# Seven half-size products in place of eight for two blocks of a mixer's input projection

## The reference, cut to what matters

```python
h = rmsnorm(x, norm_mix_g)
gq, gk, gv, gz, gb, ga, sB, sC, sx, cq, ck, cv = split_cols(h @ w_in)
...
u, sc_buf_new = causal_dwconv(sC * sx, sc_buf, sc_conv_w)
y_b = group_rmsnorm(sB * u, SC_GROUPS, sc_norm_g).astype(dt)
```

## Time and profile before

| | us |
|---|---|
| median of 3 runs | 930.41 (930.28 to 930.81) |
| the profiled execution | 930.92 |
| its span in the profile | 929.2 |
| TensorE busy in the span | 918.9 |
| VectorE busy | 651.8 |
| ScalarE busy | 443.0 |
| GpSimd busy | 164.6 |

### The profile page before, as it was taken

How to read it: one execution, slowest core, us unless ns; L and a number is a source line. 1 busy time by engine, 2 the same in 40 slices (tenths; PEclk the granted TensorE clock), 3 DMA queues, 4 the chain that set the end, 5 groups by cost and what they waited for, 6 DMA issues and landing times.

```text
span 929.2 us, 16790 instructions
## 1 busy us (share of the span) xinstructions
PE 918.9 (99%) x6895; PEld 835.2 (90%) x6895; DVE 651.8 (70%) x1060; ACT 443.0 (48%) x793; POOL 164.6 (18%) x195
## 2 busy tenths in 40 slices
PE   8999999999999999999999999999999999999998
PEld 7899888999988877798788999999999998888886
DVE  6726888866888755743667999999999998445321
ACT  7634454645675543645554534444444445333310
POOL 0072101101845330000002222122222220000000
PEclk9999999999999999999999999999999999999999
DMA  9624143124204183345705222222222224312221
GB/s 322 214 89 147 47 157 117 47 74 145 87 4 136 65 265 123 121 152 209 245 1 204 92 74 69 86 92 91 91 91 92 86 65 182 108 68 91 90 80 57
DMA packets 75490, 106.34 MB, mean 114 GB/s; under 512 B 2798, under 2 KB 54166, under 8 KB 75030
## 3 DMA queue, kind: packets, MB, share of 16 engines
q1 hardware_dynamic: 75414, 105.27, 33.8%
HBM read 94.89 MB, written 10.37 MB: 113 GB/s over the span
## 4 chain that ended last, share of the span: by engine, by line
PE 91%; DVE 4%; ACT 3%; issue 1%; DMA 1%; POOL 1%; SPq 0%; DVEq 0%; ACTq 0%
PE bank L1274 8%; PE bank L1272 8%; PE bank L1273 8%; PE bank L558 6%; PE bank L559 6%; PE bank L560 6%; PE bank L519 6%; PE bank L520 6%; PE bank L521 6%; PE bank L487 5%; PE bank L584 2%; PE bank L585 2%; PE bank L586 2%; PE bank L505 2%; PE bank L507 2%; PE bank L506 2%
## 5 line engine op out<-in xcount | busy, mean ns | idle before, releaser
L2236 DVE TENSOR_TENSOR wlo<-wraw,whi 128x2048 fp32r<-128x2048 f32 (+1 forms) x56 | 126.1, 2252 | 100.3 <-ACT whi L1681 91.7
L1681 ACT ACTIVATE whi<-wraw 128x2048 fp32r<-128x2048 f32 (+1 forms) x58 | 109.3, 1885 | 95.4 <-PE bank L560 70.2
L519 PE MATMUL bank<-hhi,whi 128*128 128x320 f32 x352 | 115.3, 328 | 0.0
L521 PE MATMUL bank<-hhi,wlo 128*128 128x320 f32 x352 | 108.7, 309 | 0.0
L520 PE MATMUL bank<-hlo,whi 128*128 128x320 f32 x352 | 108.7, 309 | 0.0
L519 PEld LDWEIGHTS bank<-hhi,whi 128*128 128x128 f32 x352 | 66.2, 188 | 4.1 <-issue 2.6
L520 PEld LDWEIGHTS bank<-hlo,whi 128*128 128x128 f32 x352 | 66.2, 188 | 1.6 <-issue 1.0
L521 PEld LDWEIGHTS bank<-hhi,wlo 128*128 128x128 f32 x352 | 66.1, 188 | 0.0
L558 PE MATMUL bank<-whi,hhi 128*128 128x512 f32 x150 | 58.4, 389 | 0.0
L559 PE MATMUL bank<-wlo,hhi 128*128 128x512 f32 x150 | 58.4, 389 | 0.0
L560 PE MATMUL bank<-whi,hlo 128*128 128x512 f32 x150 | 58.3, 389 | 0.0
(11 more groups left out here) (501 smaller groups left out, 2657.6 us busy)
## 6 DMA issues: line engine op xcount, KB each, us to landing
wraw<-in_w_in SPq DMA_DIRECT2D x13, 1024.0 KB, 5.5
wraw<-in_w_gate SPq DMA_DIRECT2D x11, 1024.0 KB, 5.1
wraw<-in_w_up SPq DMA_DIRECT2D x11, 1024.0 KB, 5.2
wraw<-in_w_down SPq DMA_DIRECT2D x10, 1024.0 KB, 5.0
kTs<-in_cache_sb_k SPq DMA_DIRECT2D x8, 512.0 KB, 4.7
vraw<-in_cache_sb_v SPq DMA_DIRECT2D x8, 512.0 KB, 5.1
wraw<-in_w_mix_out SPq DMA_DIRECT2D x4, 1024.0 KB, 7.6
kmT<-in_cache_mem_k SPq DMA_DIRECT2D x8, 512.0 KB, 6.1
```

What stands on the lines that cost most here:

```text
L519: T.matmul(o, wh[:, k, cs], hhi[:, k, hs], start=(k == 0), stop=False)
L521: ins = T.matmul(o, wl[:, k, cs], hhi[:, k, hs], start=False, stop=(k == KD - 1))
L1681: V(wv(whi, i), wv(wraw, i), ACT.Copy).then_inc(s["w_hi_ready"], 1)
L2236: V.tensor_tensor(wv(wlo, i), wv(wraw, i), wv(whi, i).bitcast(F32), ALU.subtract)\
```

## The change

Each 1024 x 256 product is cut into halves of depth, of columns and of tokens, and formed by seven products of quarters (Winograd's form of Strassen's scheme) in place of eight: four of them use sums of quarters of the weights or of the tokens. Such a product is 4 steps of k by 3 matmuls. The sums and their own high and low parts are new work for VectorE and ScalarE, and the seven results are added on VectorE. The four token sums overwrite `xT`, so TensorE's gates, which read it, move ahead of the second half of `cq`. The key and value caches for the first samples are loaded later, since the sums of the `sx` weights lie where they would land. GpSimd's list is the same.

TensorE, the seven products and their order (`FRONT_STEPS`), two steps a unit:

```diff
+        FRONT_ORDER = (2, 1, 0, 3)
+        FRONT_STEPS = (("p1", "00"), ("p7", "p6"), ("p5", "01"), ("10",))
...
+"front": (2, 6, 7), "wide": (0, 1, 2, 6, 7), "turns": (3, 4, 5, 0, 1)
...
-            across(("cq", 0), B_CQ, hhi, hlo, ready=lambda c, k: pe.wait_ge(s["hlo_ready"], k + 1) if c == 0 else None)
+            across(("cq", 0), B_CQ, hhi, hlo, cs=(0,), ready=lambda c, k: pe.wait_ge(s["hlo_ready"], k + 1))
...
+            ring[0] = "cq"
+            across(("cq", 0), B_CQ, hhi, hlo, cs=(1,))
+
+            def front_products(name, i, step):
+                wh, wl = wv(whi, i), wv(wlo, i)
+                if step == 0:
+                    lo_cut(pe, i)
+                for what in FRONT_STEPS[step]:
+                    o = bank[take((name, what), at="front" if name == "sC" else "wide")][:, 0:HALF]
+                    if what == "p1":
...
+                    elif what == "p7":
+                        pe.wait_ge(s["front_lo"], FRONT_PART[0])
+                        w, a = (corner(wh, 0, 1), corner(wl, 0, 1)), (fhi[2], front_sum(xTr, 2))
+                    elif what == "p6":
+                        pe.wait_ge(s["front_lo"], FRONT_PART[name])
+                        pe.wait_ge(s["front_lo"], FRONT_PART[1])
...
+                    for k in range(half_block):
+                        T.matmul(o, w[0][:, k, :], a[0][:, k, :], start=(k == 0), stop=False)
+                        T.matmul(o, w[0][:, k, :], a[1][:, k, :], start=False, stop=False)
+                        ins = T.matmul(o, w[1][:, k, :], a[0][:, k, :], start=False, stop=(k == half_block - 1))
+                    done(ins, (name, what))
...
             for u, (name, i, c, h) in enumerate(UNITS):
-                unit(name, i, c, h)
-                if u == 1:
+                if u < 8:
+                    front_products(name, i, u % 4)
+                else:
+                    unit(name, i, c, h)
+                if u == 0:
+                    ring[0] = "turns"
                     turn_gates()
                     turn_keys()
+                    ring[0], ring_at["woven"] = "woven", 1
```

SyncE, the caches of the first samples:

```diff
-                if i == B_SC:
-                    filled(sp, ("rx", 1))
-                    load_k(0)
-                    load_v(0)
-                    load_k(1)
-                if i == B_SX:
-                    load_v(1)
-                    for bt in range(2, 4):
+                if i == B_QKV[2]:
+                    filled(sp, ("sx", "10"))
+                    for bt in range(4):
                         load_k(bt)
                         load_v(bt)
```

ScalarE, in the order of its list:

```diff
                 V(ckv[:, t, :], bank[b][:, :], ACT.Copy, scale=rcol[:, t:t + 1]).then_inc(bank_free[b], 1)
+            def front_weights(name, i):
+                e.wait_ge(s["front_raw"], FRONT_RAW[name])
+                cut_hi(i)
+                e.wait_ge(s["front_raw"], FRONT_RAW[name] + 1)
+                V(fth[name][:, :, :, :], fraw[name][:, :, :, :], ACT.Copy).then_inc(s["front_hi"], 1)
+
+            def front_tokens(m):
+                n = FRONT_ORDER[m]
+                e.wait_ge(s["front_raw"], FRONT_SUM + (2, 3, 3, 4)[m])
+                V(fhi[n][:, :, :], front_sum(xT, n), ACT.Copy).then_inc(s["front_hi"], 1)
...
+            front_weights("sC", B_SC)
             e.wait_ge(s["small_loaded"], 16)
             e.wait_ge(s["mrow_loaded"], 32)
...
-            cut_hi(B_SC)
             e.wait_ge(s["cq_zeros"], 1)
             for c in range(2):
+                if c == 1:
+                    front_tokens(0)
+                    front_tokens(1)
...
+            front_first("sC")
+            front_tokens(2)
+            front_tokens(3)
+            front_weights("sx", B_SX)
+            keys_out()
             for u, (name, i, c, h) in enumerate(UNITS):
...
+                if u == 4:
+                    front_first("sx")
```

VectorE, in the order of its list:

```diff
             link(V.memset(qbl[:, :, :, :], 0.0))
+            def front_weights(name, i):
...
+                V.tensor_tensor(t[:, 0], corner(w, 0, 1), corner(w, 0, 0), ALU.subtract)
+                V.tensor_tensor(corner(w, 0, 1), corner(w, 1, 1), corner(w, 0, 1), ALU.subtract).then_inc(s["front_raw"], 1)
+                dve.wait_ge(s["front_raw"], FRONT_RAW[name])
+                link(V.tensor_tensor(t[:, 1], corner(w, 1, 1), t[:, 0], ALU.subtract))
+                V.tensor_tensor(t[:, 2], corner(w, 1, 0), t[:, 1], ALU.subtract).then_inc(s["front_raw"], 1)
...
+            front_weights("sC", B_SC)
+            front_weights("sx", B_SX)
             cut_lo(B_SC)
-            for c in range(2):
-                for h in range(2):
-                    evacuated(dve, (("cq", 0), c, h))
...
             for h in range(2):
                 b = filled(dve, ("gates", h))
                 V.tensor_copy(gT[:, h * HALF:(h + 1) * HALF], bank[b][:, 0:HALF]).then_inc(bank_free[b], 1)
+            front_tokens()
+            front_weights_lo("sC")
+            front_tokens_lo(0)
+            front_tokens_lo(1)
+            front_outputs("sC", 0)
+            front_tokens_lo(2)
+            front_tokens_lo(3)
+            front_outputs("sC", 1)
+            cut_lo(B_SX)
...
             for u, (name, i, c, h) in enumerate(UNITS):
...
+                if 1 < u < 8:
+                    front_outputs(name, u % 4)
+                    if u == 2:
+                        front_weights_lo("sx")
+                    if u == 3:
+                        queries_of_samples()
...
+                if u in (7, 8):
+                    short_conv(u - 7)
...
                 if u in EVENT_AT and EVENT_AT[u] < NI:
                     weights(EVENT_AT[u])
```

More of the change, by code:

```diff
@@ L334, in hybrid_step @@
         use = {}
-        rings = {"all": tuple(range(8)), "main": (0, 1, 2, 3, 4, 5), "long": (6, 7), "bulk": (0, 1, 2), "woven": (3, 4, 5), "few": (0, 1), "cq": (5, 7, 0, 1), "out": (0, 1, 2, 3, 4), "sums": (5, 6, 7), "tail": (5, 6, 7, 0, 1, 2, 3, 4), "gdn": (2, 3, 4, 5, 6, 7)}
+        rings = {"all": tuple(range(8)), "main": (0, 1, 2, 3, 4, 5), "long": (6, 7), "bulk": (0, 1, 2), "woven": (3, 4, 5), "few": (0, 1), "cq": (5, 7, 0, 1), "out": (0, 1, 2, 3, 4), "sums": (5, 6, 7), "tail": (5, 6, 7, 0, 1, 2, 3, 4), "gdn": (2, 3, 4, 5, 6, 7), "front": (2, 6, 7), "wide": (0, 1, 2, 6, 7), "turns": (3, 4, 5, 0, 1)}
         ring_at = {name: 0 for name in rings}
@@ new lines, in front_weights_lo, with front_tokens @@
+            def front_weights_lo(name):
+                dve.wait_ge(s["front_hi"], FRONT_PART[name])
+                V.tensor_tensor(ftl[name][:, :, :, :], fraw[name][:, :, :, :], fth[name][:, :, :, :].bitcast(F32), ALU.subtract)\
+                    .then_inc(s["front_lo"], 1)
+            def front_tokens():
+                raw = [front_sum(xT, n) for n in range(4)]
+                V.tensor_tensor(raw[0], raw[2], raw[0], ALU.add).then_inc(s["front_raw"], 1)
+                V.tensor_tensor(raw[2], raw[1], raw[2], ALU.subtract).then_inc(s["front_raw"], 1)
+                dve.wait_ge(s["front_raw"], FRONT_SUM + 2)
+                V.tensor_tensor(raw[1], raw[0], raw[1], ALU.subtract).then_inc(s["front_raw"], 1)
+                dve.wait_ge(s["front_raw"], FRONT_SUM + 3)
+                V.tensor_tensor(raw[3], raw[3], raw[1], ALU.subtract).then_inc(s["front_raw"], 1)
@@ new lines, in front_tokens_lo, with front_add, front_outputs @@
+            def front_tokens_lo(m):
+                n = FRONT_ORDER[m]
+                dve.wait_ge(s["front_hi"], FRONT_PART[m])
+                V.tensor_tensor(front_sum(xTr, n), front_sum(xT, n), fhi[n][:, :, :].bitcast(F32), ALU.subtract)\
+                    .then_inc(s["front_lo"], 1)
+            def front_add(name, what, out, a):
+                b = filled(dve, (name, what))
+                return b, V.tensor_tensor(out, a, bank[b][:, 0:HALF], ALU.add)
+            def front_outputs(name, step):
+                if step == 0:
+                    evacuated(dve, (name, "p1"))
+                    b, ins = front_add(name, "00", front_out(name, 0, 0), fu[:, :])
+                    ins.then_inc(bank_free[b], 1)
+                elif step == 1:
+                    b, ins = front_add(name, "p6", front_out(name, 1, 0), fu[:, :])
+                    ins.then_inc(bank_free[b], 1)
+                    evacuated(dve, (name, "p6"))
+                    b, ins = front_add(name, "p7", front_out(name, 0, 1), front_out(name, 1, 0))
+                    ins.then_inc(bank_free[b], 1)
+                    evacuated(dve, (name, "p7"))
+                elif step == 2:
+                    front_add(name, "p5", front_out(name, 1, 1), front_out(name, 0, 1))
+                    b, ins = front_add(name, "p5", front_out(name, 1, 0), front_out(name, 1, 0))
+                    ins.then_inc(bank_free[b], 1)
+                    b, ins = front_add(name, "01", front_out(name, 0, 1), front_out(name, 0, 1))
+                    ins.then_inc(bank_free[b], 1)
+                    evacuated(dve, (name, "p5"))
+                else:
```

(23 more changed lines are left out.)

67 lines of the change are left out of this document (51 added, 16 removed).

## The result

The changed kernel takes **934.42 us** (median) against 930.61 for the kernel before on the same chip; the ratio is 1.0038, with a 95% interval of 1.0027 to 1.0048. So it is slower by 0.4%, and 1.8 us above the forecast of 932.6, inside its range. One of its six runs took 1504.01 us at a mean granted clock of 0.556; it counts in the median and not in the ratio. The profiled execution took 934.39, 3.47 more than that of before.

The account below looks back on a forecast made before the run. TensorE's list plus its gaps was taken as the bound: 4.0 us removed, 0.3, 4.5, 0.4 and 1.0 added for waits, +2.2 on 930.41 gave 932.6 us, range 927.4 to 936.6.

Parts of the forecast that it names:

- The likeliest case: TensorE waits 3 to 6 us at item 0 for weights behind GpSimd's late masks; 930.9 to 934.5 us, chance 0.45.
- Removed work, 4.0 less 0.3 for VectorE: TensorE: 24 fewer matmuls save 3.6 us, five banks at `turn_keys` 0.4; VectorE's late low parts cost 0.3.
- The wait at item 0, 4.5: VectorE's long instructions hold up GpSimd's masks until 78.7 us; TensorE waits 4.5 us for item 0's weights, bounds 0 to 7.
- a rival with a chance of 0.15: Clock falls in TensorE's wait, 2.2 us more lost (934.8, up to 937); chance 0.15 together with the upper bounds.
- the main sum: Whole kernel: -4.0 + 0.3 + 4.5 + 0.4 + 1.0 = +2.2 us, giving 932.6 for the median.
- The first qkv unit's bank, 0.4: Behind item 0, the first `qkv` unit waits 0.4 us for a bank that VectorE's queued additions free.
- Items 4 and 5, 1.0: VectorE's backlog makes TensorE wait 0.7 us at item 4 and some 0.3 at item 5; 1.0 taken, range 0 to 2.
- ScalarE's new order: High parts of `sC` and its sums precede the memory rows' squares; GpSimd starts at 48.8 for 45.55; TensorE doesn't wait.
- The half-way case: GpSimd's masks end at 75 to 77 us, TensorE waits 1 to 3 us; 928.6 to 931 us, chance 0.13.
- the slip-through case: Some thirty of GpSimd's 38 mask operations done by 72 us, item 0 in time; 928.1, full cover 926.4; chance 0.27.
- the main case: Same as the likeliest case: GpSimd gets one turn per long VectorE instruction, TensorE waits 3 to 6 us; chance 0.45.

Follow-up runs that it names:

- two selects first: Changed kernel with GpSimd making the selects of items 0 and 1 ahead of the last third of its masks, the others behind; 931.24 us.
- masks behind the load: Changed kernel with GpSimd's masks moved near the start of its list, behind the load and the copy to `w8pad`; 930.92 us.
- the squares first: Changed kernel with ScalarE making the memory rows' squares ahead of the C block's weights, as in the kernel before; 932.04 us.

## Why the prediction was right, and where it was off

The likeliest case came: slower than before through a wait at item 0. Term by term:

- *Removed work, 4.0 less 0.3 for VectorE.* Right. 1.9 us were in hand at item 0 and 1.8 more by the end of `sx`, 3.7. From its first matmul to the next product's, `turn_keys` takes 1.04 us (58.41 to 59.45) for 1.41 (61.91 to 63.32), so the banks gave 0.4 and 0.3 was lost before item 0, both as taken. Timeline of TensorE, the changed kernel and then the kernel before:
```profile
58.41 1.29 PE L826 MATMUL bank<-ident,ckv 128*128 128x128 f32 x10
59.45 0.39 PE L804 MATMUL bank<-fhi,whi 128*128 128x320 f32 x1
```
```profile
63.32 0.39 PE L519 MATMUL bank<-hhi,whi 128*128 128x320 f32 x1
```
- *The wait at item 0, 4.5.* Right in mechanism, 0.7 too long. The masks ended at 78.45 for a forecast of 78.7. But the sum has a slip: 72.3 and 5.8 make 78.1, not 78.7, and by its own terms the wait would have been 3.7, next to the 3.81 measured. The count is off by one as well: the subtraction at 60.14 in the earlier trace rows (line 1554, now 1609) is the 22nd operation itself, so 17 operations, not 16, take the 5.8 us. In the changed kernel it started at 72.68, after VectorE was through at 71.8, and the 17 took 5.8 us again. TensorE came 0.3 us later than I had it, and the weights 0.25 sooner.
- *The step that failed: a sum without the clock.* I put its fall into a rival with a chance of 0.15 and left it out of the main sum. It came with the wait and cost 1.5 us, in place of the 2.2 that I took from "as long as the wait": the waits of 2.31, 2.55 and 3.81 us each lost 1.5 to 1.7 behind them. With it the sum is +3.7, and the forecast 934.1. With the slip put right too it is 933.3: the slip brought the forecast 0.8 us nearer to the result, and that part is luck.
- *The first qkv unit's bank, 0.4.* Nothing here, but it is the very wait that the run with two selects first made 2.55 us long.
- *Items 4 and 5, 1.0.* Right: from item 2's turn to line 632 at 114 us the difference grows from 1.8 to 2.8.
- *ScalarE's new order.* GpSimd started 3.2 us later (48.74 for 45.55), as forecast. Undoing it ended the masks only 0.7 us earlier, but TensorE was also 0.8 us later at item 0 (76.82 for 76.04), and the wait was 2.31 in place of 3.81. By the medians, each against the kernel before on its chip, 2.2 us came back, which fits a clock that fell in three of nine executions only.
- *The half-way case and the slip-through case* had 0.40 between them. Both needed more of GpSimd's operations done by 72 us than came: 20 were, for the 22 counted, and rows 9, on which the main case rested, held.

## What to carry to other kernels

An engine's unedited list can set the price of a change: before giving VectorE work in a stretch that it idles in, ask which engine used that idle time, and what stands behind it in that engine's list. What others wait for goes ahead of what can be late: moving eight items' selects ahead of a third of the masks turned a loss of 3.8 us into a gain of 2. And a wait of TensorE can have two prices, its length and the slow matmuls behind it.

## What the runs showed of the hardware that was not expected

- One operand is enough: a multiplication of 128x1280 values from SBUF to SBUF, 0.87 us, held GpSimd's operations of 0.2 to 0.3 us for most of its length (0.66 and 0.76 shown), like a subtraction of 1.5 us with two operands.
- Both sides pay. With 640-wide instructions of VectorE beside the masks, each of VectorE's took 1.08 us for 0.82 to 0.88, and one of GpSimd's passed in 0.7 to 1.0 (timeline of VectorE, masks behind the load):

```profile
39.05 1.08 DVE L2337 TENSOR_TENSOR hlo<-xT,hhi 128x640 fp32r<-128x640 f32 x1
```

- The granted clock is full in the trace while TensorE stands. In the changed kernel it fell about 1 us after TensorE had gone on, elsewhere from 0.1 us before it went on to 0.8 us after. In the traces it stayed full behind the waits of 0.3, 1.0, 1.2 and 1.5 us and fell behind those of 2.3, 2.4, 2.6 and 3.8; the price there was 1.4 to 1.7 us, nearly the same for the shortest as for the longest. Only one execution of each kernel has a trace, and in the others the clock didn't always fall: its mean was 1.000 in six of nine executions with the squares first and in six of eleven with two selects first. With two selects first the five executions at 0.998 were only 0.2 us longer in the mean than the six at 1.000, so the price at the spot isn't always one in the whole time; why is open.

The Trainium skill (TensorE: Matmul & The Clock Gate, What's actually happening) has an idle array drop to half its clock. The traces agree, with 0.267 us a matmul in place of 0.147.
